# Last stage of a decoder layer on one core: the add of the residual row split by columns between VectorE and Pool

## The reference

```python
y = routed_experts(h2, idx, wts, w_gate, w_up, w_down).reshape(n, l, d)   # sum of the two weighted expert rows of a token
x = x + gate2 * y                                                         # gate2: 1024 values per sequence
...
y32 = x32 * lax.rsqrt(jnp.mean(x32 * x32, axis=-1, keepdims=True) + EPS)  # final RMSNorm
return (y32 * normf_g)                                                    # y_prompt, y_sample
```

## Time and profile before

| | us |
|---|---|
| median of 3 runs | 1899.67 |
| lowest and highest of the 3 | 1894.11, 2061.77 |
| the profiled execution, its time | 1899.67 |
| its span, from the first to the last instruction | 1898.0 |
| the last stage in the span, from the first gate product to the end | 1828.66 to 1898.0 |

### The profile page before, as it was taken

One profiled execution on the slowest core, in us unless ns is written; L12 is line 12 of the kernel. 1 busy time (PEld: TensorE's weight loads), 2 busy tenths in 40 slices (PEclk: granted clock), 3 DMA queues, 4 the chain that ended last, 5 costly groups with the idle time before them and its releaser, 6 DMA issues.

```text
span 1898.0 us, 29695 instructions
## 1 busy us (share of the span) xinstructions
PE 1830.8 (96%) x9077; PEld 1381.1 (73%) x9078; DVE 1137.9 (60%) x2171; ACT 727.8 (38%) x1356; POOL 229.4 (12%) x331
## 2 busy tenths in 40 slices
PE   5999999999999999999899999999899999999987
PEld 2787778777567777777588888888477777777632
DVE  3788888888540000001655555556778888888648
ACT  3444444434330000002321221221477777777522
POOL 0100000000000000000101111101322222222111
PEclk7999999999899999999999999999999999999998
DMA  9322212222485444455844344444889869999587
GB/s 373 108 95 112 108 70 106 112 97 91 181 271 192 177 177 177 177 188 185 307 161 151 133 155 144 155 147 166 273 281 354 292 213 337 328 355 313 193 334 316
DMA packets 175851, 384.40 MB, mean 203 GB/s; under 512 B 30184, under 2 KB 104056, under 8 KB 168572
## 3 DMA queue, kind: packets, MB, share of 16 engines
q1 hardware_dynamic: 139836, 321.28, 47.8%
q0 software_dynamic: 19744, 53.89, 7.6%
q10 hardware_dynamic: 16224, 8.65, 1.5%
HBM read 296.80 MB, written 103.73 MB: 211 GB/s over the span
## 4 chain that ended last, share of the span: by engine, by line
PE 66%; DVE 3%; DMA 2%; issue 1%; ACT 1%; ACTq 0%; POOL 0%; DVEq 0%; SPq 0%; POOLq 0%
PE bank L168 18%; PE bank L170 17%; PE bank L169 17%; PE bank L2865 4%; PE bank L2830 2%; PE bank L2008 2%; PE bank L2970 1%; DMA mixer_parts<-oT_split 1%; PE bank L1307 1%; PE bank L2068 1%; DVE late_x L2807 1%; PE bank L2853 1%; DVE expert_down L2802 0%; DMA gathered<-weighted_rows 0%; DMA expert_down<-weighted_rows 0%
## 5 line engine op out<-in xcount | busy, mean ns | idle before, releaser
L168 PE MATMUL bank<-w_mix_hi,hT_hi 128*128 128x512 f32 (+3 forms) x544 | 203.2, 374 | 3.8 <-DVE hT_lo L610 2.5
L1216 DVE SCALAR_TENSOR_TENSOR ma_rows<-tanh_rows,bank 128x512 f32<-128x512 f32 x32 | 20.6, 684 | 310.2 <-PE bank L170 159.9
L2728 DVE TENSOR_TENSOR gate_up_lo<-expert_gate_up,gate_up_hi 128x2048 fp32r<-128x2048 f32 x86 | 196.4, 2288 | 10.9 <-ACT gate_up_hi L2588 9.9
L169 PE MATMUL bank<-w_mix_hi,hT_lo 128*128 128x512 f32 (+3 forms) x544 | 198.8, 365 | 0.0
L170 PE MATMUL bank<-w_mix_lo,hT_hi 128*128 128x512 f32 (+3 forms) x544 | 198.3, 365 | 0.0
L2588 ACT CAST gate_up_hi<-expert_gate_up 128x2048 fp32r (+1 forms) x86 | 165.1, 1923 | 69.0 <-issue 67.2
L168 PE MATMUL bank<-gate_up_hi,gathered_T_hi 128*128 128x512 f32 x352 | 142.5, 405 | 4.9 <-DVE gathered_T_lo L2719 2.1
L170 PE MATMUL bank<-gate_up_lo,gathered_T_hi 128*128 128x512 f32 x352 | 138.4, 393 | 0.0
L169 PE MATMUL bank<-gate_up_hi,gathered_T_lo 128*128 128x512 f32 x352 | 137.9, 392 | 0.0
L168 PEld LDWEIGHTS bank<-w_mix_hi,hT_hi 128*128 128x128 f32 (+1 forms) x544 | 100.6, 185 | 37.0 <-issue 20.3
L170 PEld LDWEIGHTS bank<-w_mix_lo,hT_hi 128*128 128x128 f32 (+1 forms) x544 | 100.6, 185 | 19.1
(11 more groups left out here) (463 smaller groups left out, 3833.9 us busy)
## 6 DMA issues: line engine op xcount, KB each, us to landing
expert_gate_up<-in_w_gate SPq DMA_DIRECT2D x33, 1024.0 KB, 9.6
expert_gate_up<-in_w_up SPq DMA_DIRECT2D x33, 1024.0 KB, 13.1
expert_down<-in_w_down SPq DMA_DIRECT2D x32, 1024.0 KB, 12.7
h_parts<-hT_split SPq DMA_DIRECT2D x16, 1024.0 KB, 5.1
mixer_parts<-oT_split SPq DMA_DIRECT2D x32, 512.0 KB, 8.2
w_ada_part<-in_w_ada SPq DMA_DIRECT2D x16, 1024.0 KB, 10.7
h_parts_b<-hT_split SPq DMA_DIRECT2D x16, 1024.0 KB, 4.9
expert_down<-weighted_rows SPq DMA_DIRECT2D x12, 1024.0 KB, 8.2
```

Source lines behind the costliest of these rows:

```text
L168: nc_mm(out, left[0], right[0], start=first, stop=False)
L169: nc_mm(out, left[1], right[0], start=False, stop=False)
L1216: last = nc.vector.scalar_tensor_tensor(out=ma[:, par, at], in0=tg[:, at], scalar=1.0, in1=ps[2 + n][:, :], op0=ALU.add, op1=ALU.mult)
L2728: nc.vector.tensor_tensor(wg[par][1][:, at], ring[:, bass.ds(slot * GU + n * HG, HG)], wg[par][0][:, at].bitcast(F32), ALU.subtract).then_ ...
```

## The change

The add of the residual rows is cut by columns. VectorE now adds columns 0 to 639 (by_vector), Pool columns 640 to 1023 (by_pool). Pool's part is a new function add, called for each tile ahead of rms. It waits for the same semaphore as VectorE's part (weighted: the gate products of the tile are there), and for the loads of residual rows and gates at the tiles where these are first needed. It counts up a semaphore of its own, added (the semaphore counted of an earlier part, used again from a value of 17). Whoever waited for summed now waits for added too: SP before the load of tile i + 4, and ACT before square(i).

```diff
@@ -2359,6 +2359,8 @@
     paired, weighted, summed = sem("c_paired"), sem("c_weighted"), sem("c_summed")
     sumsq, mean, root, done = ready["sumsq"], ready["mean"], ready["root"], sem("c_done")
     BEFORE = NT + 1
+    added = ready["counted"]
+    by_vector, by_pool = slice(0, 640), slice(640, D)
     xc, (gate, gate_s, gf) = late_rows(ring, ready["spare_rows"])
     sq = ring[:, 3 * D:4 * D]
     pair = [downs[:, n * DOWN:(n + 1) * DOWN].rearrange("p (k d) -> p k d", k=2) for n in range(3)] + [xg[:, :, :]]
@@ -2486,6 +2488,7 @@
         for i in range(NT):
             sp.wait_ge(summed, i + 1)
             if i + NB <= NT:
+                sp.wait_ge(added, BEFORE + i + 1)
                 pairs(sp, i + NB, P if i + NB < NT else MS)
         for slot in range(4):
             wait_apart(sp, idx_in[slot], (fore * 2 + 2 + (8 - slot)) // 4 * 16, passed)
@@ -2552,7 +2555,16 @@
             pool.wait_ge(mean, BEFORE + i + 1)
             pool.tensor_tensor(t[0:m, k, 2:3], t[0:m, k, 1:2], minus_half[0:m, :], ALU.pow).then_inc(root, 1)
 
+        def add(i, m):
+            pool.wait_ge(weighted, i + 1)
+            if i in (0, NX):
+                wait_apart(pool, late_in[i // NX], 16 * NX, passed)
+            if i == NT:
+                wait_apart(pool, gates_in, 64, passed)
+            pool.tensor_tensor(xc(i, m)[:, by_pool], xc(i, m)[:, by_pool], pair[i % NB][0:m, 0, by_pool], ALU.add).then_inc(added, 1)
+
         for i, m in tiles():
+            add(i, m)
             rms(i, m)
         wait_apart(pool, stored[0], fore * 16 + 48, passed)
         wait_apart(pool, stored[1], fore * 16 + 32, passed)
@@ -2698,6 +2710,7 @@
             if i:
                 act.wait_ge(sumsq, BEFORE + i)
             act.wait_ge(summed, i + 1)
+            act.wait_ge(added, BEFORE + i + 1)
             nc.scalar.activation(sq[0:m, :], xc(i, m), ACT.Square, accum_out=t[0:m, i % NB, 0:1]).then_inc(sumsq, 1)
 
         def store(i, m):
@@ -2804,7 +2817,7 @@
             if i == NX:
                 dve.wait_ge(late_in[1], 16 * NX)
             dve.wait_ge(weighted, i + 1)
-            nc.vector.tensor_tensor(xc(i, m), xc(i, m), pair[k][0:m, 0, :], ALU.add).then_inc(summed, 1)
+            nc.vector.tensor_tensor(xc(i, m)[:, by_vector], xc(i, m)[:, by_vector], pair[k][0:m, 0, by_vector], ALU.add).then_inc(summed, 1)
 
         def norm(i, m):
             dve.wait_ge(root, BEFORE + i + 1)
```

## The result

| | before | changed |
|---|---|---|
| median, us | 1899.67 | 1906.77 (1904.64 to 1907.33, 5 runs) |
| ratio, 95% interval | | 1.0042 (1.0028 to 1.0057) |
| span of the profiled execution | 1898.0 | 1904.7 |

The change makes the kernel slower by 0.42% (0.28 to 0.57): about 8 us, with an interval from 5.3 to 10.8. 1907.5 was forecast. What follows tells how far the steps bear out the number.

A forecast was written before the change was run, and what follows sets the result against it. TensorE bounds the whole kernel, DVE's 3.66 us round the changed stage, with PE and DMA close behind. 15 longer rounds (+7.3) and the last tile (+0.5) gave +7.8 us: 1907.5, range 1897 to 1914.

The forecast's parts named there:

- DVE's round bounds the stage, PE and DMA just behind: Last stage, per tile: DVE 3.66 us, PE 3.60, DMA 3.69; the measured mean round was 3.74.
- 384 columns fewer save 0.40 us: DVE's add: at 1.05 ns a column it falls from 1.14 to 0.74 us, start to start.
- Exclusion, in both directions: DVE instructions with two SBUF inputs and Pool reads of SBUF block each other; no exclusion: -2.2 us, chance 0.15.
- Pool goes ahead of the norm: After DVE's add, Pool's older request goes first; rival, DVE keeps its turn: +9 to +10 us, chance 0.20.
- Block of 0.97 us, round 4.23: DVE stands still for Pool's 0.87 us add plus 0.1 handing over; 15 rounds at 4.23 instead of 3.74 cost +7.3 us.
- +0.5 us at the end: Last tile, start of gate products to whole add: 3.03 us instead of 2.52.
- +7.8 in all: Total over the stage, 15 longer rounds plus the last tile: span 1905.8, time 1907.5.
- What would show it: Signs: Pool's add at 1.6 to 1.8 us or 0.7 late, norm starting about 1 us later, DMA share near 0.87.
- Later loads cost nothing: Loads issued about 0.5 us later after the gate products still fit: the buffer's ring needs 3.71 us a tile.
- Clock: Rival: PE idling lowers TensorE's granted clock to the 1.2 GHz level, PE becomes the bound, +53 us, 1953; chance 0.04.

The follow-up runs named there:

- a trial: Short VectorE and Pool instructions behind the last norm of the kernel before; here VectorE's add, after a wait, met a running 1024-column Pool add: 2.41 us instead of 0.76.
- Pool's extra add: Kernel before, VectorE's full add kept, plus a 128x384 Pool add per tile that no other engine waits for; ratio to before 1.0054 (1.0034 to 1.0074).
- the first experiment: Changed kernel without Pool's add and the waits for it, columns 640 to 1023 left unadded; 1895.9 us, ratio to before 0.9989 (0.9974 to 1.0005).

## Why the prediction was right

- *DVE's round bounds the stage, PE and DMA just behind.* Right: taking 0.40 us from DVE alone brought the mean round from 3.74 to 3.62 only. PE's 3.60 was a little high: it is the duration of eight products with the overlap into the next tile, and without Pool's add tiles followed each other at 3.43 us.
- *384 columns fewer save 0.40 us.* Right: 1.14 to 0.74.
- *Exclusion, in both directions.* Right, and the half for which no row stood, that DVE is held up too, is now shown: 0.74 in the norm, 2.41 for 0.76 us in a trial, 2.05 for 1.23 us where Pool's extra add began first. Without Pool, or with one input in PSUM, the norm keeps its time.
- *Pool goes ahead of the norm.* Right for tiles 1 to 15, wrong for tile 16. The reason given, that the older request goes first, is not the rule: in tile 16, too, Pool's add is recorded as started before the norm.
- *Block of 0.97 us, round 4.23.* Too dear. The add alone takes 1.00 (0.87 was put), but it blocks for 0.74 only: the fixed part of 0.19 passes while Pool waits, and no hand-over is to be seen. The round is 3.99, so the 15 rounds cost 3.7 us by the trace's round instead of 7.3. They came to 4.3 in the trace, 0.4 of it DVE waiting for one pair.
- *+0.5 us at the end.* Too cheap: 1.67, since DVE kept its turn.
- *+7.8 in all.* Of the 6.7 between the profiled spans 6.0 lie in the stage; the rounds were priced 3.0 too high and the end 1.2 too low, and 0.73 came from ahead of the stage by chance. That 1907.5 stands 0.7 from 1906.77 is partly luck: the mechanism and the sign were right, and its sizes off in opposite directions. The 6.0 us of the stage are also 2 less than the 8 of the ratio; they lie inside its interval, and no row accounts for the rest.
- *What would show it.* Pool's add at 1.6 to 1.8 us came (1.63). The norm's start 1 us behind DVE's add did not: it is recorded as starting at once and lasting longer. DMA's share in mid stage was 0.94 to 1.02, not 0.87, at a round of 3.99 instead of 4.23.
- *Later loads cost nothing.* Nearly: PE waited up to 1.8 us for a pair, of which DVE felt 0.4.
- *Clock.* It stayed at 1.00 from 1828 to 1892, also where PE was busy for only 2.47 of 4 us:

```profile
1844.00:1848.00 4.00, 2.47 (x7) 0.81 (x5) 3.97 (x5) 1.16 (x3) 2.37 (x3) 1.00 0.96 316
```

## What to carry to other kernels

Moving part of a VectorE instruction to a Pool instruction that reads SBUF can help only if Pool's part runs beside VectorE instructions with at most one input in SBUF. Beside two, VectorE stands still while Pool reads, and here Pool needs 2.1 ns a column for what VectorE does in 1.05. Such a loss shows as a longer busy instruction, not as idle time, so compare mean durations by shape before and after. And before an engine is relieved, take its work away without replacement, as in the first experiment: it tells what the relief can bring at all, here 0.1%, hardly told from nothing.

## What the runs showed of the hardware that was not expected

- Pool's turn depends on VectorE's rows. With an instruction of 640 columns on few rows followed, without a wait, by one of more rows, both with two SBUF inputs, Pool is kept out for both (2.76 us for an add of 1.00); with equal or fewer rows it gets in between (1.63). A semaphore wait between the two gives Pool its turn (1.62). With 1024 columns in the first, 32 and then 128 rows, Pool got in without a wait, once (2.10 us, the norm 2.08), so the full rule is open.
- A recorded start is not a claim. A Pool add shown from 0.5 us before VectorE's add was still held up by it (3.45 instead of 2.35 us). The Trainium skill says in "SBUF — State Buffer", section "SBUF: two separate sides", that whichever starts first gets the ports for the whole instruction; the trials agree where VectorE's instruction came from a wait for a semaphore, but not always where it was queued right behind another one, and there the measurement decides.
- Pool's two-input add in float32 takes 0.19 us and 2.1 ns a column, and the same on 32 rows as on 128 (0.98 against 1.00 us for 384 columns).
